# A hybrid trunk step on one core: down products of the feed-forward blocks as 2x2 block products in 7 multiplications

## The reference

```
x = x + 0.5 * (silu(n(x) @ Wg1) * (n(x) @ Wu1)) @ Wd1      # n = RMSNorm with gain
p = n(x) @ W_in                                            # q, k, v, gates of 4 mLSTM and 4 retention heads
y = [sigmoid(o) * GN(mLSTM(q,k,v,i,f)), silu(g) * GN(retention(rope(q),rope(k),v))]
x = x + y @ W_out
x = x + 0.5 * (silu(n(x) @ Wg2) * (n(x) @ Wu2)) @ Wd2
return n(x), and the states C, n, m, R after the last frame
```

## Time and profile before

| | |
|---|---|
| median of 3 runs | 1065.37 us (1064.82 to 1065.58) |
| span of the profiled execution, first to last instruction | 1063.2 us |
| around it, to the median (the profiled execution has no time of its own beside its span) | 2.2 us |
| busy, of the span | PE 99%, DVE 64%, ACT 44%, POOL 18% |
| DMA | 127.8 MB, mean 120 GB/s |
| granted TensorE clock, mean | 0.998 |
| first block: standard units, pair steps, down, pair steps, down | 12.0 to 61.2, to 145.5, to 217.8, to 323.1, to 383.4 us |
| second block, the same | 685 to 729.4, to 813.6, to 885.9, to 991.2, to 1056 us |

### The profile page before, as it was taken

One profiled execution on the slowest core, in us unless ns is written; L12 is line 12 of the kernel. 1 busy time (PEld: TensorE's weight loads), 2 busy tenths in 40 slices (PEclk: granted clock), 3 DMA queues, 4 the chain that ended last, 5 costly groups with the idle time before them and its releaser, 6 DMA issues.

```text
span 1063.2 us, 20510 instructions
## 1 busy us (share of the span) xinstructions
PE 1055.5 (99%) x8425; PEld 1052.1 (99%) x8425; DVE 684.2 (64%) x1170; ACT 465.7 (44%) x822; POOL 189.8 (18%) x169
## 2 busy tenths in 40 slices
PE   9999999999999999999999999999999999999997
PEld 8999999999999999999999999999999999999997
DVE  6997752367866676655655556598875236777555
ACT  6466641256652345433222224446664114666323
POOL 1122100112201211210332222212210002220111
PEclk9999999999999999999999999999999999999999
DMA  8589482479833377445454224547958328892422
GB/s 225 121 172 200 100 196 84 96 159 177 176 82 96 64 135 139 71 68 80 69 80 75 67 78 62 140 91 170 206 110 187 92 82 166 178 180 52 124 75 84
DMA packets 245493, 127.84 MB, mean 120 GB/s; under 512 B 9228, under 2 KB 243892, under 8 KB 245272
## 3 DMA queue, kind: packets, MB, share of 16 engines
q1 hardware_dynamic: 207032, 106.79, 41.6%
q0 software_dynamic: 38288, 19.72, 14.6%
q10 hardware_dynamic: 80, 0.02, 0.0%
HBM read 123.22 MB, written 3.29 MB: 119 GB/s over the span
## 4 chain that ended last, share of the span: by engine, by line
PE 98%; DMA 1%; DVE 0%; SPq 0%; issue 0%; ACT 0%
PE dense L623 52%; PE dense L768 31%; PE core_banks L768 5%; PE core_banks L623 3%; PE dense L691 1%; PE core_banks L928 1%; PE core_banks L943 1%; PE dense L824 1%; PE core_banks L946 1%; PE core_banks L918 1%; DMA x_tok<-in_x_prompt 1%; PE core_banks L955 0%; PE core_banks L912 0%; PE core_banks L914 0%; PE core_banks L805 0%; PE core_banks L666 0%
## 5 line engine op out<-in xcount | busy, mean ns | idle before, releaser
L1481 DVE TENSOR_TENSOR w_lo<-w_raw,w_hi 128x1024 fp32r<-128x1024 f32 (+2 forms) x118 | 131.7, 1133 | 55.1 <-ACT w_hi L1068 55.0
L1068 ACT ACTIVATE w_hi<-w_raw 128x1024 fp32r<-128x1024 f32 (+2 forms) x118 | 105.2, 904 | 89.3 <-PE dense L623 81.4
L623 PE MATMUL dense<-h_hi,w_hi 128*128 128x272 f32 x684 | 142.5, 290 | 0.0
L623 PE MATMUL dense<-xg_hi,w_hi 128*128 128x272 f32 x672 | 142.2, 293 | 0.0
L623 PE MATMUL dense<-h_lo,w_hi 128*128 128x272 f32 x684 | 141.1, 287 | 0.0
L623 PE MATMUL dense<-h_hi,w_lo 128*128 128x272 f32 x684 | 140.9, 287 | 0.0
L623 PE MATMUL dense<-xg_lo,w_hi 128*128 128x272 f32 x672 | 138.9, 288 | 0.0
L623 PE MATMUL dense<-xg_hi,w_lo 128*128 128x272 f32 x672 | 138.8, 287 | 0.0
L768 PE MATMUL dense<-x_op_hi,w_lo 128*128 128x272 f32 x432 | 124.6, 289 | 0.0
L768 PE MATMUL dense<-x_op_hi,w_hi 128*128 128x272 f32 x432 | 124.5, 288 | 0.0
L768 PE MATMUL dense<-x_late_hi,w_lo 128*128 128x272 f32 x432 | 124.5, 288 | 0.0
(11 more groups left out here) (341 smaller groups left out, 2212.1 us busy)
## 6 DMA issues: line engine op xcount, KB each, us to landing
w_raw<-in_w_ffn_up SPq DMA_DIRECT2D x91, 256.0 KB, 3.6
w_src<-in_w_ffn_gate SPq DMA_DIRECT2D x90, 256.0 KB, 4.6
w_raw<-in_w_in SPq DMA_DIRECT2D x32, 512.0 KB, 8.9
w_raw<-in_w_ffn_down SPq DMA_DIRECT2D x32, 384.0 KB, 4.0
w_raw<-in_w_ffn_down SPq DMA_DIRECT2D x32, 320.0 KB, 3.5
w_src<-in_w_ffn_gate POOLq DMA_DIRECT2D x36, 256.0 KB, 5.2
w_raw<-in_w_ffn_up POOLq DMA_DIRECT2D x36, 256.0 KB, 5.8
w_raw<-in_w_out SPq DMA_DIRECT2D x8, 512.0 KB, 3.9
```

What stands on the lines that cost most here:

```text
L623: last = nc.tensor.matmul(out[:, half, 0:TH], w[:, s % 4, k, :], x(kt)[:, half * TH:(half + 1) * TH], start=start and n == 0 and m == 0, s ...
L1068: nc.scalar.activation(w_hi[:, s % 4, 0:k_tiles(s), :], raw, ACT.Copy).then_inc(w_hi_ready, 1)
L1481: nc.vector.tensor_tensor(w_lo[:, s % 4, 0:nk, :], w_raw[:, s % RAW, 0:nk, :], w_hi[:, s % 4, 0:nk, :].bitcast(F32), ALU.subtract).then_in ...
```

## The change

- Inner tiles come in three chunks, 8, 8 and 6 (`FC`); the pair steps are split accordingly, 4, 8 and 6 (`PAIRS`).
- The down products of the first two chunks are block products too: `down_pair`, four steps of 84 matmuls per chunk, each for two output tiles. `down_quarter` takes every second inner tile of the chunk. Loads, accumulating DMAs, sums, w_hi and w_lo of these steps are those of pair steps, and all steps of a block are counted in one row (STEPS = 26).
- Each product of a down step is added to xT straight from its bank by VectorE (`take_down`, 272 wide, seven a step), at once.
- The third chunk (6 tiles, `TAIL_TILES`) goes by standard products, one unit for an output tile (`down`).
- The down steps need h as seven operands for every group of two inner tiles (`h_op`, hi and lo). Operands 3, 6 and 0 are h blocks as they are (`H_COPIES`), 1, 2, 5 and 4 sums (`H_SUMS`), which GpSimd forms (`sum_h`). ScalarE makes all hi parts (`h_to_hi`), VectorE the lo parts of the copies (`h_to_lo`), GpSimd those of the sums (`sums_to_lo`); for the last group of a chunk VectorE makes all seven.
- The tile `kept` is gone. ScalarE copies products 0, 1 and 2 into the gate and h tiles themselves; products 4 and 5 are read by VectorE in their banks, and product 6 waits for VectorE's second take.
- In the first down step TensorE's products go in the order 0, 1, 3, 2, 4, 5, 6, with the last k tile of 0, 1 and 3 left to the end of them, and 5 cut in two around 4.
- Two of the four 1088-wide x sums are made by GpSimd (`make_late_sums`). In the first block ScalarE squares xT in the tail.

The core of the diff:

```diff
-    PAIRS = (range(0, 8), range(8, 18))
-    FC, F0 = (12, FT - 12), (0, 12)
+    PAIRS = (range(0, 4), range(4, 12), range(12, 18))
+    FC, F0 = (8, 8, FT - 16), (0, 8, 16)
...
+    H_OPS = (3, 6, 0, 1, 2, 5, 4)
+    H_SUMS = (1, 2, 5, 4)
+    H_COPIES = (3, 6, 0)
+    def lo_by_dve(k):
+        return H_OPS if k % GROUPS == GROUPS - 1 else H_COPIES
...
             def pair(n, c, p):                                  # TensorE
                     if o == 6:
-                        pe.wait_ge(product_copied, 4 * P_ + 4)
+                        if e == 0:
+                            pe.wait_ge(pair_gate_made, 3 * Q + 2)
+                        else:
+                            pe.wait_ge(pair_up_taken, 3 * Q + 2)
...
+            def down_pair(n, c, d):                             # TensorE
+                if d >= 2:
+                    pe.wait_ge(down_taken, BLOCKS * (D - 1))
+                elif d == 1:
+                    pe.wait_ge(pair_h_made, 2 * (pair_index(n, PAIRS[c][-1]) // 2 + 1))
+                else:
...
+                    for o in OPENS:
+                        pe.wait_ge(block_lo, BLOCKS * g + o + 1)
+                        part(o, range(last_k))
+                    for o in OPENS:
+                        h_ready(n, before + 1, o)
+                        part(o, range(last_k, KH)).then_inc(product_done, 1)
+                    pe.wait_ge(down_taken, BLOCKS * D + 1)
+                    pe.wait_ge(block_lo, BLOCKS * g + 3)
+                    h_ready(n, before + 1, 2)
+                    part(2, range(KH)).then_inc(product_done, 1)
+                    pe.wait_ge(down_taken, BLOCKS * D + 2)
+                    pe.wait_ge(block_lo, BLOCKS * g + 6)
+                    part(5, range(KH // 2))
+                    pe.wait_ge(down_taken, BLOCKS * D + 4)
+                    h_ready(n, before + 1, 4)
+                    part(4, range(KH)).then_inc(product_done, 1)
...
+                    part(5, range(KH // 2, KH)).then_inc(product_done, 1)
+                    pe.wait_ge(down_taken, BLOCKS * D + 5)
...
+                for o in range(BLOCKS):
+                    if o in (2, 4, 6):
+                        pe.wait_ge(down_taken, BLOCKS * D + o - 1)
+                    pe.wait_ge(block_lo, BLOCKS * g + o + 1)
+                    part(o, range(KH)).then_inc(product_done, 1)
...
             def up_second(n, p):                                # VectorE
-                dve.wait_ge(product_copied, 4 * pair_index(n, p) + 4)
-                nc.vector.tensor_tensor(pair_h[1][:, TH:T], kept[:, 1, 3, :], kept[:, 1, 1, :], ALU.add)
+                dve.wait_ge(product_done, done_by(step_of_pair(n, p), 4))
+                dve.wait_ge(product_copied, 3 * pair_index(n, p) + 2)
+                out = pair_h[1][:, TH:T]
+                nc.vector.tensor_tensor(out, pair_banks(1)[0], out, ALU.subtract).then_inc(pair_up_taken, 1)
...
             def pair(n, c, p):                                  # VectorE
                     if o == 4:
                         if e == 0:
                             gate_first(n, p, Q)
-                            if p - 2 in PAIRS[c]:
-                                pair_h_to_lo(c, p - 2, Q - 1, 1)
                         else:
                             up_first(n, p)
                     if o == 5:
...                                                              # gate_second or up_second, as before
-                    next_lo(n, c, p, o)
+                    if follows and c < 2 and o == 2:
+                        for h_o in H_COPIES:
+                            h_to_lo(n, group_of(p) - 1, h_o)
+                    if follows and c == 2 and o in (4, 6):
+                        tail_to_lo(n, p // 2 - 1, 1 if o == 4 else 0)
+                    next_lo(n, g, o)
                     if e and o == 4:
                         up_first_gated(Q)
...
+            def down_pair(n, c, d):                             # VectorE
+                if d == 0:
+                    up_last(n, PAIRS[c][-1], pair_index(n, PAIRS[c][-1]) // 2)
+                    sum_t2(g + 1)
+                    for o in (3, 6, 0, 1, 2):
+                        h_to_lo(n, k, o)
+                    take_down(n, c, d, 0)
+                    h_to_lo(n, k, 5)
+                    h_to_lo(n, k, 4)
+                    take_down(n, c, d, 1)
+                    take_down(n, c, d, 3)
+                    next_lo(n, g, 0)
+                    next_lo(n, g, 1)
+                    take_down(n, c, d, 2)
...
+                for o in range(BLOCKS):
+                    take_down(n, c, d, o)
+                    if o == 0:
+                        sum_t2(g + 1)
+                    if o == 3:
+                        sum_t4(g + 1)
+                    next_lo(n, g, o)
...
+            def sum_h(n, k):                                    # GpSimd
+                x11, x21, x12, x22 = (pair_h[m][:, half * TH:(half + 1) * TH] for m in range(2) for half in range(2))
...
+                nc.gpsimd.tensor_tensor(h_source(k, 1), x22, x21, ALU.subtract).then_inc(h_summed, 1)
...                                                              # 2 from 1, 5 from 2, and 4 = x11 + x21
+            def sums_to_lo(n, k):
+                for o in H_SUMS:
+                    pool.wait_ge(h_op_hi_ready, BLOCKS * group_index(n, k) + H_OPS.index(o) + 1)
+                    hi, lo = h_op[:, k % GROUPS, 0, o, :], h_op[:, k % GROUPS, 1, o, :]
+                    nc.gpsimd.tensor_tensor(lo, h_source(k, o), hi.bitcast(F32), ALU.subtract).then_inc(h_op_lo_pool, 1)
...
+            def sums_between(n, g):                             # after add_blocks(g)
+                for c in range(2):
+                    for p in PAIRS[c][1::2]:
+                        up, k = step_of_pair(0, p), group_of(p)
+                        if i == up + 2:
+                            sum_h(n, k)
+                        if i == up + 3 and o_sums_by_pool(k):
+                            sums_to_lo(n, k)
```

More of the change, by code:

```diff
@@ L702, in ffn @@
                 plain(n, norm)
-                for c in range(2):
+                for c in range(3):
                     for p in PAIRS[c]:
                         pair(n, c, p)
-                    down(n, c)
+                    if c < 2:
+                        for d in range(DOWNS):
+                            down_pair(n, c, d)
+                down(n)
             def plain(n, norm):
@@ L761, in pair @@
                     if p == 0:
                         pe.wait_ge(x_op_ready, BLOCKS * n + o + 1)
-                    pe.wait_ge(block_lo, BLOCKS * P_ + o + 1)
-                    hi, lo = block_of(w_hi, n, o), block_of(w_lo, n, o)
+                    pe.wait_ge(block_lo, BLOCKS * g + o + 1)
                     x_hi, x_lo = x_op(x_op_hi, x_late_hi, o), x_op(x_op_lo, x_late_lo, o)
-                    for k in range(KH):
-                        for m, (w, x) in enumerate(((hi, x_hi), (hi, x_lo), (lo, x_hi))):
-                            last = nc.tensor.matmul(banks[BANK[o]], w[:, k, :], x[:, k, :], start=o in OPENS and k == 0 and m == 0,
-                                                    stop=k == KH - 1 and m == 2, skip_group_check=o not in OPENS)
@@ L1061, in split_hi @@
                 unit = down_unit(s)
-                if unit is not None and unit[2] < 4:
-                    act.wait_ge(product_done, BLOCKS * pair_index(unit[0], PAIRS[unit[1]][-1]) + min(2 * unit[2] + 2, BLOCKS))
+                if unit is not None and unit[1] < 4:
+                    act.wait_ge(product_done, BLOCKS * step_of_pair(unit[0], NP - 1) + min(2 * unit[1] + 2, BLOCKS))
                 elif s >= 4:
@@ L1106, in block_to_hi @@
-            def block_to_hi(n, p, o):
-                e, P_ = p % 2, pair_index(n, p)
-                c = int(p >= PAIRS[1][0])
+                first_pair(n)
+                for c in range(3):
+                    for p in PAIRS[c]:
+                        if p:
+                            pair(n, c, p)
+                    if c < 2:
+                        for d in range(DOWNS):
+                            down_pair(n, c, d)
+                tail_to_hi(n, NP // 2 - 1, 1)
+                tail_to_hi(n, NP // 2 - 1, 0)
@@ new lines, in copy_product @@
+                if o == 0 and e == 0 and Q:
+                    act.wait_ge(pair_h_made, 2 * Q - 1)
+                if o == 0 and e:
+                    if p // 2 > chunk_start(2):
+                        act.wait_ge(tail_h_lo, TAIL_TILES * n + 2 * (p // 2 - chunk_start(2)))
+                    else:
+                        act.wait_ge(h_op_lo_dve, dve_los(n, group - 1))
+                        act.wait_ge(h_summed, len(H_SUMS) * group_index(n, group))
+                act.wait_ge(product_done, done_by(step_of_pair(n, p), o))
@@ L1505, in ffn @@
                 plain(n, norm)
-                for c in range(2):
-                    if c == 0:
-                        first_pair(n)
-                    else:
```

(9 more changed lines are left out.)

712 lines of the change are left out of this document (427 added, 285 removed).

## The result

The kernel after took 1181.96 us, the median of 4 runs (1178.39 to 1184.59), against 1065.28 us for the kernel before on the same chip: ratio 1.109, 95% interval 1.1066 to 1.1114. The prediction had the direction right and the size wrong: 11% slower, not 3.9%, and outside the range.

What follows compares the result with a forecast made beforehand. TensorE, busy 99% of the span, was taken to bound the kernel. 1065.4 - 24.1 saved + 65.4 of waits (A 16.2, B 4.8, C 18.4, D 16.0, E 10.0) gave 1106.7, say 1107 us, 3.9% slower; range 1079 to 1122.

Steps and rivals of the forecast that it cites:

- Matmuls saved: TensorE has 96 fewer matmuls in each block, 192 in all: 24.1 us saved.
- A: Product 6 of each up step waits for VectorE's second take: 0.90 us in each of 18, 16.2 us.
- B: Product 6 waits likewise in gate steps without h sums: 0.54 us in 4, 0.64 in 4, 4.8 us.
- C: Gate steps with h sums (8): GpSimd's adds hold up VectorE, TensorE waits 2.3 us each, 18.4 us.
- E: First gate step (2): product 6 waits for a packed VectorE, 5.0 us each, 10.0 us.
- D: First down step of a chunk (4): waits for h operands and takes, 4.0 us each, 16.0 us.
- The covered waits (2): Rival: in every pair step product 4's reader is done before TensorE reaches product 6; faster, 1056 us; chance 11%.
- The chain without blocking (1): Rival: GpSimd's short operations slip between VectorE's, all terms take their lower ends, 1082 us; chance 13%.
- GpSimd's lateness (3): Rival: GpSimd 1.5 us later than counted, so `sum_t2` waits for its DMA in some 16 steps, 1131 us; chance 7%.

Runs made afterwards that it cites:

- Experiment 1: The kernel after, with VectorE's second take straight after its first, before w_lo of block 4, in every pair step but the first: 1159.89 us, ratio 1.0883.
- experiment 3: The kernel before, with product 6 also waiting for VectorE's second take and nothing else of the change: 1106.98 us, ratio 1.0387.
- Experiment 2: The kernel after, with GpSimd's four remainders (`sums_to_lo`) waiting for the end of the gate step: 1137.46 us, ratio 1.0673.
- Experiment 7: The kernel after, with GpSimd's remainders of groups 0 and 1 moved to after the end of the first step: 1179.86 us, ratio 1.1079.
- experiment 4: The kernel after, with TensorE running matmuls that nobody reads where it would wait long: 1159.85 us, ratio 1.0883.
- experiments 8 and 9: Both from the 1075.6 us version: 8 spreads GpSimd's group 0 remainders and gives group 1's to VectorE, 1077.17 us; 9 keeps three edits, 1080.7 us.
- The best, 1075.6 us: As experiment 5, with the h sums of each chunk's last group made by VectorE in place of GpSimd: 1075.61 us, ratio 1.0111.
- experiment 5: The kernel after, with the orders of VectorE's and GpSimd's queues altered and no operation added or removed: 1082.45 us, ratio 1.0165.
- experiment 9: The 1075.6 us version, with GpSimd's group 0 remainders after the second step and two takes reordered in first down steps: 1080.7 us, ratio 1.0144.

## Why the prediction was right in sign and wrong in size

**Matmuls saved: right.** 192 fewer; the twelve further down steps last 10.56 us on average. The saving is real, but every version loses more than that in its steps.

**A and B: right.** 0.87 us of wait against 0.90, 0.52 and 0.65 against 0.54 and 0.64. Experiment 1 removes them by the place in the queue alone, experiment 3 makes such waits in the kernel before (1.14 and 0.79 us). I counted 18 waiting up steps; they are 16, since the last of each block has no w_lo in front of its take, so the waits of A sum to 13.9 us. Its other 7.9 us are slower spacing, some 6 of it the lower clock that an up step inherits from the gate step before it (11.5 us for an up step by itself, up to 12.9 behind one of these).

**C: the step that failed.** It cost 63.4 us and not 18.4, 45 of the 78 us by which the span grew more than I said. I counted "four adds of 0.72 between them" and let the other four, "later four more (`sums_to_lo`)", cost nothing ahead of `gate_second`. They came onto the w_lo of block 2, which stands ahead of `gate_second`. Two things were wrong. The moment: GpSimd's two DMA issues of 205.87 and 206.67 overlap each other and the burst, which begins at 207.45. And "the two engines take turns", read from two operations in the earlier trace rows: here the four in a row left VectorE no turn, 4.13 us for a w_lo of 0.68. Experiment 2 takes the burst from this place and the term becomes 2.35 us. What makes the engines alternate at one place (77.08, and the bursts of experiment 2) and not at another stays open. A DMA issue of GpSimd runs directly ahead of each burst that held VectorE off in a gate step, but one also runs ahead of the burst of 62.89, where they alternate. The size was off too: beside VectorE's work an add of 272 columns lasts 0.84 to 1.2 us, where I took 0.72, a little more than half of the 1.36 us for 544 in the earlier trace rows. That this didn't matter by itself is seen in experiment 2, where the sums of `sum_h` last as long and the term is 2.35.

The Trainium skill, SBUF — State Buffer, "Who interferes with whom", which I cited at C, agrees with this trace in which operations contend: VectorE's takes from PSUM keep their 0.43 us beside GpSimd's work (80.41), operations with two SBUF operands stretch. It would have put the time near 1115 us by my working. The miss was in how many of GpSimd's operations fall on VectorE, and when.

**E: the upper end that I named, exceeded.** I allowed 10 us "if the backlog of the standard units arrives too" and took 5.0. It arrived: the eviction at 67.81 instead of 61.28, a burst at 62.89 in front of it, two waits (3.95 before product 2, 6.36 before product 6), 13.5 us. Experiment 7 shows the part of the remainders, 4.5 us of it; how the rest divides was not tried.

**D: right in kind, 5.0 for 4.0**, of which 1.4 is slower spacing. Its waits are 3.6 us, inside 2.0 to 4.7.

**The clock: not in the prediction at all.** It cost 22 us by experiment 4, most of the 27.8 us of slower spacing, and lies inside the terms above. I counted a wait as its own length. The longest wait in the earlier trace rows is 1.1 us, so the trace of before had no row of what follows a long one.

**Rivals.** The covered waits (2) are out: product 6 waits in every pair step, but for the last up step of each block. The chain without blocking (1) is out too: it had 0.62 us for a gate step with sums, which costs 7.92, and 2.35 even in experiment 2. GpSimd's lateness (3) had the right engine and the wrong sign: VectorE has no wait for a DMA, so GpSimd wasn't late with these, it was early with its remainders. It did come late in experiments 8 and 9.

No version beat the kernel before. The best, 1075.6 us, keeps 29.4 us of excess against 24.1 saved, and some 5 us elsewhere. It stays open whether an order exists in which the second and first down steps lose 11 us more.

## What to carry to other kernels

Saving work on the engine that is 99% busy pays only if the readers that free its buffers keep their lead: list for each product which engine's queue its release stands in, and what stands ahead of it there. When work is put on GpSimd, ask at which moment it becomes ready and what VectorE does then, not only how much it is; and when it is delayed, ask what stands behind it in GpSimd's own queue. A wait of a few us can cost more than its length on TensorE.

## What the runs showed of the hardware

- Four GpSimd operations of 272 columns with two SBUF operands and no waits between them held off VectorE's w_lo, which also has two, for their whole length (4.13 us for 0.68), in all eight gate steps with h sums. At 77.08 in the same kernel, and in the eight bursts that experiment 2 moved, such four alternated with VectorE, one operation each. What decides between the two was not tried.
- A take of VectorE from PSUM kept its 0.43 us beside GpSimd's burst (80.41).
- A GpSimd add of 272 columns took 0.84 to 1.2 us beside VectorE's work in the gate steps with h sums and the first down steps.
- Behind waits of 2.6 us and more in the kernel after TensorE ran at the granted clock of 0.50, 1.2 GHz, for a while: 95.5 us in all (6.8 of it at the kernel's end), 11.3 with the waits filled by matmuls, and 22 us of the kernel's time. It isn't the length of the wait alone: in experiment 2 the clock fell behind two of the eight waits of 2.06 us, and in experiment 5 it didn't fall behind one of 2.63 us.
- A DMA that GpSimd issued behind a delayed burst kept VectorE idle for 5.38 us (experiment 9).
